# A two-layer hybrid mixer and expert trunk: attention values, attention weights and the final state moved between other products, and layer 0's first input block summed by halves of its weights

## The reference

```python
def token_mixers(hn, l, p, ctx):
    proj = jnp.einsum('bld,de->ble', hn, p['w_in'][l])
    (da_q, da_k, da_v, r_q, r_k, r_v, r_g, g_q, g_ff, g_fb, g_i, g_g) = _split_columns(proj)
    ...
    o_da = diff_attention(q, k, v, lam)              # (softmax(q1 k1) - lam softmax(q2 k2)) v
    ...
    o_ret, sr_f, sr_b = bidir_recurrence(rq, rk, rk, rv, ..., RET_CHUNK)
    o_ret = rmsnorm(o_ret, p['ret_norm'][l]) * jax.nn.silu(r_g...)
    ...
    o_hg, sh_f, sh_b = bidir_recurrence(hq, one_minus_f(zf), one_minus_f(zb), hv, log_f(zf), log_f(zb), ...)
    mixed = jnp.concatenate([o_da, o_ret, o_hg], axis=-1)
    out = jnp.einsum('blm,md->bld', mixed, p['w_out'][l])

def layer(x, cond, l, p, ctx):
    mod = jnp.einsum('...d,de->...e', jax.nn.silu(cond), p['w_ada'][l]) + p['b_ada'][l]
    sh1, sc1, g1, sh2, sc2, g2 = jnp.split(mod, 6, axis=-1)
    hn = rmsnorm(x, p['norm_mix'][l]) * (1.0 + sc1) + sh1
    mix, ctx_tensors = token_mixers(hn, l, p, ctx)
    x = x + g1 * mix
    hn = rmsnorm(x, p['norm_ffn'][l]) * (1.0 + sc2) + sh2
    x = x + g2 * moe(hn, l, p)
```

## Time and profile before

| what | us |
|---|---|
| median of 3 runs (lowest, highest) | 923.29 (917.27, 923.44) |
| the profiled execution | 920.11 |
| its span, first to last instruction | 918.3 |
| TensorE busy | 875.0 (95%) |
| VectorE busy | 456.5 (50%) |
| ScalarE busy | 165.5 (18%) |
| mean granted TensorE clock | 0.992 |

### The profile page before, as it was taken

The page is one execution under the profiler, slowest core; times in us unless marked ns, Lnnn a source line. Parts: engine busy times, 40 slices in busy tenths (PEclk is TensorE's granted clock), DMA queues, the critical chain, the costliest instruction groups (busy, mean ns, idle before and its releaser), DMA issues.

```text
span 918.3 us, 13341 instructions
## 1 busy us (share of the span) xinstructions
PE 875.0 (95%) x4774; PEld 447.5 (49%) x4774; DVE 456.5 (50%) x839; ACT 165.5 (18%) x428; POOL 79.6 (9%) x110
## 2 busy tenths in 40 slices
PE   5799999999989999999999999999999999999997
PEld 1555566558743333333337455756874333333332
DVE  2395887753573223232236887876356323323222
ACT  2202015221201111100121301442120111110111
POOL 1113130000010000000011223000001000000001
PEclk9999999999999999999999999999999999999999
DMA  9998666759789999999997555474578999999992
GB/s 360 411 395 314 229 232 229 307 207 385 285 331 416 421 420 419 421 421 420 421 413 317 221 216 206 184 293 189 235 279 318 416 420 419 421 421 420 419 420 116
DMA packets 50317, 307.37 MB, mean 335 GB/s; under 512 B 8682, under 2 KB 8698, under 8 KB 16848
## 3 DMA queue, kind: packets, MB, share of 16 engines
q1 hardware_dynamic: 42368, 291.52, 78.5%
q0 software_dynamic: 4848, 12.40, 3.7%
q10 hardware_dynamic: 3040, 2.62, 0.9%
HBM read 305.46 MB, written 4.73 MB: 338 GB/s over the span
## 4 chain that ended last, share of the span: by engine, by line
PE 81%; DVE 9%; DMA 5%; ACT 2%; issue 2%; SPq 1%; DVEq 0%; ACTq 0%
PE ps L479 77%; PE ps L514 4%; DMA wT<-in_w_in 3%; DMA ring<-in_w_experts 2%; ACT eP L1702 1%; DVE fa L1267 1%; DVE rt L1138 1%; DVE stat L1138 0%; SPq L392 0%; PE ps L546 0%; DVE proj L1601 0%; DVE eP L1448 0%; DVE xy L1273 0%; DVE x L1685 0%; DVE hnT L1192 0%
## 5 line engine op out<-in xcount | busy, mean ns | idle before, releaser
L479 PE MATMUL ps<-ring,proj 128*64 128x512 f32 x1024 | 284.5, 599 | 2.0 <-ACT proj L1954 1.7
L479 PE MATMUL ps<-ring,hnT 128*128 128x512 f32 (+1 forms) x576 | 204.5, 506 | 2.4 <-DVE hnT L1522 1.1
L479 PEld LDWEIGHTS ps<-ring,proj 128*64 128x64 f32 x1024 | 88.0, 137 | 138.2 <-issue 138.2
L479 PEld LDWEIGHTS ps<-ring,hnT 128*128 128x128 f32 x576 | 106.7, 191 | 76.8 <-issue 68.9
L1669 DVE COPY proj<-ps 128x512 f32<-128x512 f32 x16 | 11.1, 691 | 131.1 <-PE ps L479 131.1
L479 PE MATMUL ps<-home_ra,proj 128*64 128x512 f32 x128 | 57.6, 593 | 3.4 <-issue 3.4
L479 PE MATMUL ps<-ring,silT 128*32 128x512 f32 x384 | 46.8, 608 | 12.3 <-DVE silT L1155 6.6
L479 PE MATMUL ps<-home_kd,proj 128*64 128x512 f32 x128 | 57.7, 593 | 0.0
L479 PE MATMUL ps<-home_qc,proj 128*64 128x512 f32 x128 | 57.6, 593 | 0.0
L1655 DVE RECIPROCAL proj<-proj 128x512 f32<-128x512 f32 x16 | 53.6, 3353 | 0.6
L1654 DVE TENSOR_SCALAR proj<-proj 128x512 f32<-128x512 f32 x16 | 6.8, 427 | 80.8 <-ACT proj L1702 80.8
(11 more groups left out here) (271 smaller groups left out, 1055.7 us busy)
## 6 DMA issues: line engine op xcount, KB each, us to landing
ring<-in_w_experts SPq DMA_DIRECT2D x128, 1024.0 KB, 14.1
ring<-in_w_ada SPq DMA_DIRECT2D x48, 1024.0 KB, 8.4
ring<-in_w_in SPq DMA_DIRECT2D x24, 1024.0 KB, 8.3
home_qc<-in_w_experts SPq DMA_DIRECT2D x16, 1024.0 KB, 13.0
home_ra<-in_w_experts SPq DMA_DIRECT2D x16, 1024.0 KB, 16.5
home_kd<-in_w_experts SPq DMA_DIRECT2D x16, 1024.0 KB, 18.0
ring<-in_w_out SPq DMA_DIRECT2D x8, 1024.0 KB, 10.8
eP<-in_w_experts SPq DMA_DIRECT2D x4, 1024.0 KB, 10.4
```

Source lines behind the costliest of these rows:

```text
L479: ins = nc.tensor.matmul(*a, **k)
```

## The change

Layer 0's block `f` is summed by `by_half`: for each half of the features, both head pairs and both groups, 128 columns a product, each half behind a wait for its own load only. The two banks are first set to zero, and all products accumulate. In the mixers of both layers `da_values(0, 0)` goes behind the first product block of `s`, `da_weights(1, 1)` goes behind the first half of the second `s` block and takes banks 4 and 5, and `end_state(0, "r", T_RV)` goes ahead of the first output products, behind the transposes of group 0. The code of the other engines is unchanged.

```diff
+                def by_half(name, b):
+
+                    ss, banks = [], [b]
+                    for half in range(2):
+                        ss.append(slot(RING + half))
+                        for p in range(2):
+                            if p and not half:
+                                banks.append(next_bank())
+                            if not half:
+                                mm(ps[:, banks[p], :], zeros[:, 0:P], zeros[:, 0:BLK], start=True, stop=False, skip_group_check=True)
+                            for g in range(NG):
+                                if not p:
+                                    wait_for_input(g, half)
+                                for hl in range(2):
+                                    h = 2 * p + hl
+                                    for k in range(KH * half, KH * (half + 1)):
+                                        for d in range(2):
+                                            col = 64 * h + 256 * d
+                                            last = mm(ps[64 * d:64 * d + 64, banks[p], 256 * hl + P * g:256 * hl + P * (g + 1)], by_k(ss[half], 512)[:, k % KH, col:col + 64], hnT[:, k, tok(g)], start=False, stop=(k == KC - 1), skip_group_check=True)
...
-                def da_weights(g, p):
+                def da_weights(g, p, banks=None):
...
-                        bank_of_transposes(("wPT", g, p, i), srcs, next(turn_of_banks))
+                        bank_of_transposes(("wPT", g, p, i), srcs, banks[i] if banks else next(turn_of_banks))
...
                 if not l:
                     stream_zeros(b, 5)
-                ss = open_block("f")
-                by_head_and_group("f", 0, ss, b)
-                by_head("f", 1, ss)
+                    by_half("f", b)
+                else:
+                    ss = open_block("f")
+                    by_head_and_group("f", 0, ss, b)
+                    by_head("f", 1, ss)
...
-                da_values(0, 0)
 
                 ss = open_block("s")
                 b = by_token("s", 0, 0, ss)
+                da_values(0, 0)
                 ret_scores(0)
...
                 modulation_by_feature(l, 1, next(turn_of_banks))
-                da_weights(1, 1)
                 bank_of_transposes(("rkd",), [rkT[:, hp, tok(0)] for hp in range(2)], next(turn_of_banks))
                 b = by_token("s", 1, 0, ss)
+                da_weights(1, 1, (4, 5))
                 ret_values(0)
...
                 out_slots = [[slot(), slot()]]
+                end_state(0, "r", T_RV)
                 copied_group("mix", 0)
                 out_of(0, 0)
                 out_of(1, 0)
                 transposed("mix", "mixed", 1)
-                end_state(0, "r", T_RV)
```

More of the change, by code:

```diff
@@ L661, in by_head_and_group @@
                     last.then_inc(c.fills(b, "projP", name, p), 1)
+                def by_half(name, b):
[16 more added lines that the diff above has]
+                                            last = mm(ps[64 * d:64 * d + 64, banks[p], 256 * hl + P * g:256 * hl + P * (g + 1)], by_k(ss[half], 512)[:, k % KH, col:col + 64], hnT[:, k, tok(g)], start=False, stop=(k == KC - 1), skip_group_check=True)
+                                            if not (half and g and hl and k == KC - 1 and d):
+                                                pay(last)
+                            if half:
+                                last.then_inc(c.fills(banks[p], "projP", name, p), 1)
+                    owed.extend(ss)
                 def queries_by_head_pair(ss):
```

## The result

The changed kernel runs in 927.85 us (median of 20 runs, 924.69 to 929.40) against 919.65 us (20 runs, 916.63 to 923.83). The medians are 8.2 us apart; the ratio of executions taken side by side is 1.0079 with a 95% interval of 1.0064 to 1.0093, some 7 us slower, where I forecast 3. The time lies in the range and the change is under 1%, but the single terms were off in both directions, and partly cancelled. The profiled execution took 928.41 us, its span is 926.6 us against 918.3, so the two traces have 8.3 us to explain.

A forecast was written before the change was run, and what follows sets the result against it. TensorE, busy 95% of the span, was taken as the bound, with idle waits and half-clock stretches. -3.8 - 0.1 - 0.1 + 2.0 + 3.2 + 1.7 = +2.9 us on 921.0 gave 924.0 us, range 916 to 931.

The forecast's parts named there:

- Block `f`, -3.8 us: Layer 0: block starts at 31.2 us, ends at 45.4 against 49.19, gaining 3.8 us, 1.7 of it the slow stretch.
- can the 3.8 us be passed on: After layer 0's block `f`: block `a`'s first load and `queries()` both just fit, so everything after shifts by 3.8 us.
- a new wait for a DMA near 57 us: Sign that the forecast is wrong: TensorE newly waits for a load near block `a` in layer 0.
- Rival 1: Block `f`'s gain passes only partly (slow stretch stays, block `a`'s load or `queries()` late): 925.6 to 927.7 us; chance 0.18.
- The slack that I gave to `queries()`: Layer 0, ahead of `diagonal`: `queries()` stays near 66.5 us while `diagonal` moves to 67.5; 1 us of slack.
- The finer products cost nothing: Block `f`'s second pair: 128 records of 128 columns cost 7.0 us, against 7.04 us for 64 of 256.
- rival 1b: Block `f`'s second pair is bound by its weight loads, up to 4.5 us more: 928.4 us; chance 0.02.
- `da_values` and `da_weights`, -0.1 us each layer: Around the `s` blocks: values cost nothing, weights gain 0.1 us a layer; layer 0's slow stretch is left in.
- `end_state`, +2.0 and +3.2 us: Ahead of output products: waits for bank 2, losing 2.0 us in layer 0, 3.2 in layer 1, plus 1.7 clock there.
- The expert stage, taken to shift as a whole: Expert turns: loads start when TensorE releases slots, so an earlier shift carries the whole stage; 0 us added.
- Rival 3: Idle stretches of 2 us suffice for the lower clock, three more at 1.7 us, `f` -2.1: 928 to 929 us; chance 0.15.
- Rival 2: The moved end state finds its bank free and fills 0.93 and 1.12 us: 914.5 to 917 us; chance 0.12.

The follow-up runs named there:

- es_only: The kernel before, with only the end state moved ahead of the first output products: 920.58 us, ratio 1.0008 to the kernel before.
- sv: The kernel before, with only `da_values(0, 0)` and `da_weights(1, 1)` moved: 921.64 us, ratio 1.0000.
- a_only: The kernel before, with only block `a` taking its two weight slots one after the other, block `f` as it was: 920.54 us, ratio 1.0014.
- f_only: The kernel before, with only layer 0's block `f` summed half by half: 918.75 us, ratio 0.9997.
- f_split: f_only, with block `a` taking its two slots one after the other, so its first twelve records need the first load only: 917.97 us, ratio 0.9973.
- es_back: The changed kernel, with the end state back behind the transposes of group 1: 920.81 us, ratio 1.0012 to the kernel before.
- rv5: The changed kernel, with group 1's retention values in bank 5, so the early end state finds bank 2 free: 920.0 us, ratio 0.9997 to the kernel before.
- zeros: The changed kernel, with nine products of zeros into bank 4 ahead of the end state's wait: 924.81 us, ratio 1.0050 to the kernel before.
- f_split_es: f_split with the end state moved ahead of the output products, values and weights in their old places: 916.99 us, ratio 0.9981 to the kernel before.
- best: rv5 with block `a` taking its slots one after the other: 919.55 us, ratio 0.9995 to the kernel before.

## Why the prediction was right, and where only its sum was

**Block `f`, -3.8 us: the step "can the 3.8 us be passed on" failed.** The times inside the block held (31.2 forecast, 31.19 measured; 45.4 and 45.8). So did the 1.7 us of clock in it: the four traces with the old block (before, es_only, sv, a_only) have a stretch at the lower clock there, the eight with the new one none. I compared block `a`'s first load with its start and found 0.7 us of slack. But `open_block` waits for two loads, and the second, issued by SP only when a slot comes free, lands at 59.3 us. I hadn't looked at the second at all; 51.12 + 8.5 = 59.6 us against `a`'s start at 60.86 stood in the trace of before, and shows that at most 1.3 us could pass. That an issue 3.4 us earlier lands only 0.3 us earlier completes it. The prediction's own sign of being wrong, a new wait for a DMA near 57 us, is the 1.93 us ahead of 59.46. Rival 1 had the direction, a load of block `a` that comes late, but for the first load, and its reason for the upper end, "all 3.8 us would be lost only if both followed pair 0 later than now", was wrong: they went to a third thing. f_only shows it (0.9997), f_split lifts it (0.9973). The slack that I gave to `queries()` was there (66.85 us against 67.85 in f_split).

**The finer products cost nothing: right.** 128 records on `wT` take 7.16 us, 56 ns each. That also ends rival 1b. By the rule of the Trainium skill, TensorE: Matmul & The Clock Gate, section Back-to-back issue gap (some 81 ns for such a product), they would take 10.4 us by estimate; the trace disagrees.

**`da_values` and `da_weights`, -0.1 us each layer: right in time, open in the clock.** sv is at 1.0000. VectorE's 0.9 us in layer 1 is in es_back and sv (1.99 and 1.95 us for 1.12). I left layer 0's slow stretch at 187 us in the sum as unsettled; it isn't in the changed kernel's trace, -1.7 us, and what took it away isn't shown.

**`end_state`, +2.0 and +3.2 us: the mechanism was right, its clock term was mis-sized.** The waits are 2.23 and 3.65 us, for the instruction that was named. es_back and rv5 show that they are the loss, and rv5 that it is the bank and not the place. I gave the lower clock to layer 1 alone, since 2.1 us of idle time were less than the 2.98 that I had seen a stretch behind. It came in both, 1.7 us each, and in zeros' trace both are gone.

**The expert stage, taken to shift as a whole: 0.9 us off in layer 0.** Just ahead of the seventh turn (425.88 us) 0.80 us of waiting for a DMA are new. f_split, rv5, a_only and f_split_es have such a wait (0.5 to 0.8 us), the kernel before, f_only, es_back, es_only, sv and best not, zeros 0.17 us; I have no cause that sorts them, and it stays open. In layer 1 it doesn't shift as a whole either: of the twelve traces ten have a wait of some 1.2 us at the seventh turn, and the two without it (before, a_only) are the two with a slow stretch near 715 us. They come late and then don't wait, so most of that stretch's 1.7 us seems not to be in their time.

**The sum.** -3.8 became +0.3, -0.1 became -1.9, +2.0 became +3.9, 0 became +0.9, the rest 0.2 or 0.3 off each: 8.3 us between the profiled executions, some 7 by the ratio, where 2.9 were forecast. Two things made this look better than it was, and both are luck: the 1.7 us of a slow stretch that I had left in and that wasn't there, and the base of 921.0 from four executions, 1.4 us above the median of 20. So 924.0 was only 3.9 us low. Rival 1's upper end (927.7) and rival 3's lower one (928) came nearest in time. Rival 3 has half of its reasons: its slow stretches behind gaps of 2 us are there, the one in layer 1's `s` block wasn't in this trace, and its -2.1 us for `f` wasn't either. Rival 2's free bank is what rv5 built, and there its two losses vanish, without the gain that it promised on top.

## What to carry to other kernels

When a block starts earlier, look at every load that the next block waits for, the last of them first, and at whether the DMA engines are full, and with whose loads: an earlier issue then lands hardly earlier, and taking the slots one by one can let the gain through (2.15 us earlier in the trace; 0.9997 became 0.9973). When work moves between claims of a rotating set of banks, write down anew which bank each step gets and who frees it: two moves that are each free cost 6 us together, and one bank number took it back. Count an idle TensorE stretch of 2 us as possibly 1.7 us more, and give it a range in each place. Ahead of a stage that waits for loads, a slow stretch can cost much less than its 1.7 us.

## What the runs showed of the chip

The granted clock doesn't follow the length of the idle stretch just before it. Behind 1.93 us (the changed kernel, block `a`) it fell to 1.2 GHz for some 3.4 us; behind 2.07 us (f_only) and 1.99 us (es_back, layer 1) it stayed at 2.4 GHz; behind 0.73 us, with 1.03 us a little earlier, it fell in best, and behind 0.74 and 1.02 us it didn't in rv5. With nine products of zeros in the gap it stayed up in both places where it had fallen without them, in one execution. From 240 to 255 us seven of the twelve traces have one or two such stretches, in no relation to the edits that I can see. So a difference of 2 us between two profiles, one execution each, is no evidence without the timed runs.

With the DMA engines full, the time from issue to landing isn't a property of the load: the same 1024 KB took 11.6 us when issued at 47.73 us and 8.5 us when issued at 51.12. What SP's queue won by the earlier issue, GpSimd's lost (0.70 MB from 50 to 54 us in place of 1.14).
